# Attention of a two-block model: each head's weights divided in the head's own step, the output projection's parts at three places of a step

## The chip, the cores and the metric

The kernel runs on one core of a Trainium2 chip. The metric is the device time of one execution in microseconds (us), the median of several runs. The core has five engines that each work through their own list of instructions and wait for one another by semaphores: TensorE (PE, matmuls and transposes, with the weight loads PEld beside them), VectorE (DVE), ScalarE (ACT), GpSimd (POOL) and SyncE (SP, which issues most DMAs).

## The reference, cut to what matters

Two blocks are computed on a sequence of 512 tokens of 1024 channels, all in float32: a block with a Mamba-2 layer and an attention layer, then a block with two gated feed-forward layers and a second mixer. The change is in the attention layer:

```
def causal_block_attention(q_nope, q_rope, k_nope, k_rope, v):
    for i in range(S // Q_BLOCK):            # four blocks of 128 queries
        s = (q_nope . k_nope + q_rope . k_rope) * scale      # keys up to the block's end
        p = softmax(where(mask, s, -inf))
        outs.append(einsum('bhqk,bkhd->bqhd', p, v[:, :kv_len]))

def mla_mixer(...):                          # 16 heads, q and k of 96, v of 64
    o = causal_block_attention(q_nope, q_rope, k_nope, k_rope, v)
    o = o.reshape(Bsz, S, MLA_HEADS * V_HEAD) * silu(gate)
    return o @ w_out                         # 1024 x 1024
```

## The kernel before

All weight matrices come in units of at most 128x1024 numbers, 512 KB, through four buffers `raw`. A unit is split into a high part `wr` (on ACT, for a few units on DVE, L1494) and a low part `wl` (DVE, L1499, for the units of attention POOL), three buffers each; activations are split likewise into `XR` and `XL`. A float32 product is three matmuls, R by R, R by L and L by R (`three`, L743 to L745).

Attention is a loop of 18 **steps**, h = 0 to 17, written out on each engine. Head h gets its scores in step h and its transposes in step h + 2, so that steps 16 and 17 only finish heads 14 and 15. What each engine does in step h, in its order:

- PE: `turn_most(h-2)` transposes two of the three pieces of head h-2's weights `PP` (8 transposes, L960, into PSUM banks 5 and 6); `scores(h)` (banks 2, 3 and 4, L955 with the mask L956); `turn_rest(h-2)`, the third piece (2 transposes, again into bank 5, which the first piece must have left); `project(h)`, a part of the query and key projections for the heads of the next group, from a table `head_steps`: one tile of queries (9 matmuls of 512 columns), of keys (6) or both (15), and none from step 13 on; the parts of the output projection that `OUT_PARTS` names for h; and in odd steps from 3 on `values(j)` for heads h-3 and h-2, 16 matmuls (L984) into bank 7.
- ACT: `turned(h-2)`, three copies out of banks 5, 6 and 5 into `PT` (L1341); the division of blocks 0 to 2 of head h-1's weights by their sums (three multiplications by the reciprocal, L1356, after a wait on `s_tot`); the four exponentials of head h (L1365, with the sums), after a wait on `s_low`; in some steps the high part of a weight unit; in odd steps the high part of the output pair (`XR` from `OT`, L1186).
- DVE: the reciprocal of head h-1's sums (L1911, after a wait for its four exponentials); the row maxima of head h (four, L1919) and their negative (L1922, `s_low`); block 3 of head h-1's weights times the reciprocal (L1927); the evictions of `project(h)` into `QT` (three or four instructions for a tile of queries) and `KH` (two for a tile of keys), each time preceded by the casting of a unit where one is due; in odd steps the gated output `OT` (L1936) and, after ACT's high part, the low part `XL` (L1515).

`turn_most(h)` on PE waits for both halves of the division (`s_pwa`, `s_pwd`), `turn_rest(h)` for ACT's copy of the first piece (`s_pt`), `scores(h+1)` for the exponentials of head h (`s_exp`), which empty the same banks.

`OUT_PARTS` names pairs (n, t): the three matmuls of input tile t for output tile n, which need the output pair t. Before, the parts stand after `project(h)` in steps 13 to 16, ahead of `turn_most` in step 17, and after the loop (key 18). The rest of the output projection follows.

## Time and profile before

| what | us |
|---|---|
| median of 3 runs | 1834.27 (1833.46 to 1834.52) |
| the profiled execution's own time | 1834.76 |
| its span, first to last instruction | 1833.0 |
| attention, from the first score (496.20) to the end of the last parts (626.40) | 130.20 |
| PE busy in that stretch | 126.93 |
| DVE busy, ACT busy in it | 94.37, 83.08 |

The span is the stretch between the first and the last instruction that the profiler recorded; the time of the execution has 1.8 us more. A busy PE is a PE that has a matmul in flight: matmuls overlap, so one of 512 columns is listed with 0.39 us though the next starts 0.23 us after it. For that reason gaps on PE are best read from starts.

A row of a stretch gives the stretch, its length, the busy us and instructions of PE, PEld, DVE, ACT and POOL, the granted clock of TensorE as a share of 2.4 GHz, the DMA engines' busy share and GB/s. A row of a timeline gives start, duration, engine, line, operation, what it writes and reads, and how many instructions are merged in it; in brackets stands the idle time before it and what ended it.

### The profile page before, as it was taken

The page shows a single profiled execution, that of the slowest core. Times are in us where ns is not written, and L with a number is a line of the kernel's source. Part 1 is how long each engine was busy: PE and PEld are TensorE (multiplying, and loading weights), DVE is VectorE, ACT ScalarE, POOL GpSimd, SP SyncE. Part 2 cuts the span into 40 slices and gives each one's busy share as a digit, 9 for nine tenths or more (in the row PEclk, how much of TensorE's full clock was granted, in tenths as well). Part 3 has the DMA queues.
Part 4 walks back from the last instruction along what each step waited for, and adds up shares of the span by engine and source line. Part 5 has one row for each costly group of instructions (what it writes and reads, how often), then busy time and mean ns, then how long its engine had stood idle before and what let it go on. Part 6 is the DMA issues. An engine that isn't in the chain of part 4 may idle for free.

```text
span 1833.0 us, 21200 instructions
## 1 busy us (share of the span) xinstructions
PE 1804.8 (98%) x8390; PEld 1458.3 (80%) x8390; DVE 1041.9 (57%) x1511; ACT 725.3 (40%) x1198; POOL 49.6 (3%) x108
## 2 busy tenths in 40 slices
PE   8999999999999999999999999999999999999998
PEld 6767777888766788888888888888888888888887
DVE  7888887557587565444433356554444554444334
ACT  4876776434366543323222333222222332232221
POOL 1001010000210000000000000000000000000000
PEclk9999999999999999999999999999999999999999
DMA  4221222322210123333333323332332323333331
GB/s 168 79 70 58 81 70 70 103 93 82 86 47 24 60 79 109 99 92 103 86 103 99 121 77 96 97 104 92 95 101 92 101 94 93 103 93 91 104 96 55
DMA packets 48194, 163.44 MB, mean 89 GB/s; under 512 B 5344, under 2 KB 7776, under 8 KB 48096
## 3 DMA queue, kind: packets, MB, share of 16 engines
q1 hardware_dynamic: 47088, 161.24, 28.4%
q8 instruction: 67, 1.10, 0.3%
q10 hardware_dynamic: 1008, 0.85, 0.1%
q14 instruction: 31, 0.25, 0.0%
HBM read 159.97 MB, written 2.10 MB: 88 GB/s over the span
## 4 chain that ended last, share of the span: by engine, by line
PE 94%; DVE 4%; ACT 1%; issue 1%; DMA 0%; DVEq 0%; ACTq 0%
PE pb L743 28%; PE pb L744 28%; PE pb L745 28%; PE pb L846 2%; PE pb L955 2%; PE pb L960 1%; PE pb L984 1%; PE pb L1115 1%; PE pb L1117 1%; PE pb L1116 1%; DVE wl L1499 1%; PE pb L757 0%; DVE CV L1670 0%; PE pb L1125 0%; PE pb L811 0%
## 5 line engine op out<-in xcount | busy, mean ns | idle before, releaser
L743 PE MATMUL pb<-XR,wr 128*128 128x512 f32 x1584 | 625.8, 395 | 8.4 <-DVE XL L1517 8.4
L744 PE MATMUL pb<-XL,wr 128*128 128x512 f32 x1584 | 618.4, 390 | 0.0
L745 PE MATMUL pb<-XR,wl 128*128 128x512 f32 x1584 | 618.2, 390 | 0.0
L1499 DVE TENSOR_TENSOR wl<-raw,wr 128x1024 fp32r<-128x1024 f32 (+1 forms) x297 | 358.3, 1206 | 355.6 <-ACT wr L1173 354.8
L1173 ACT ACTIVATE wr<-raw 128x1024 fp32r<-128x1024 f32 (+1 forms) x295 | 305.5, 1036 | 314.6 <-PE pb L745 288.9
L743 PEld LDWEIGHTS pb<-XR,wr 128*128 128x128 f32 x1584 | 298.4, 188 | 72.8 <-issue 11.5
L745 PEld LDWEIGHTS pb<-XR,wl 128*128 128x128 f32 x1584 | 298.1, 188 | 62.9
L744 PEld LDWEIGHTS pb<-XL,wr 128*128 128x128 f32 x1584 | 298.4, 188 | 60.5
L743 PE MATMUL pb<-ffn2HR,wr 128*128 128x512 f32 (+1 forms) x198 | 72.5, 366 | 0.0
L744 PE MATMUL pb<-ffn2HL,wr 128*128 128x512 f32 (+1 forms) x198 | 72.3, 365 | 0.0
L745 PE MATMUL pb<-ffn2HR,wl 128*128 128x512 f32 (+1 forms) x198 | 72.3, 365 | 0.0
L743 PE MATMUL pb<-ffn1HR,wr 128*128 128x512 f32 x176 | 68.5, 389 | 0.0
L744 PE MATMUL pb<-ffn1HL,wr 128*128 128x512 f32 x176 | 68.5, 389 | 0.0
L745 PE MATMUL pb<-ffn1HR,wl 128*128 128x512 f32 x176 | 68.5, 389 | 0.0
L1182 ACT ACTIVATE SQ<-H 128x512 f32<-128x512 f32 x34 | 21.5, 631 | 92.3 <-DVE H L1681 47.6
L1670 DVE SCALAR_TENSOR_TENSOR CV<-U,vec,CV 128x512 f32<-128x512 f32 x72 | 54.1, 752 | 2.5
L1401 ACT ACTIVATE ffn2HR<-ffn2UP 128x512 fp32r<-128x512 f32 x22 | 13.9, 633 | 97.1 <-DVE ffn2UP L2004 97.1
L743 PE MATMUL pb<-YR,wr 128*128 128x512 f32 x128 | 50.0, 391 | 0.0
L745 PE MATMUL pb<-YR,wl 128*128 128x512 f32 x128 | 49.8, 389 | 0.0
L744 PE MATMUL pb<-YL,wr 128*128 128x512 f32 x128 | 49.8, 389 | 0.0
L1401 ACT ACTIVATE ffn1HR<-ffn1UP 128x512 fp32r<-128x512 f32 x22 | 13.9, 633 | 90.4 <-DVE ffn1UP L2004 90.4
L1759 DVE TENSOR_TENSOR LL<-LL,CB 128x1024 f32<-128x1024 f32 (+1 forms) x64 | 48.4, 819 | 0.7 <-ACT LL L1238 0.7
(337 smaller groups left out, 2248.2 us busy)
## 6 DMA issues: line engine op xcount, KB each, us to landing
raw<-in_ffn_in SPq DMA_DIRECT2D x88, 512.0 KB, 3.5
raw<-in_mix_in SPq DMA_DIRECT2D x48, 512.0 KB, 3.5
raw<-in_ssm_in SPq DMA_DIRECT2D x40, 512.0 KB, 3.3
raw<-in_ffn_out SPq DMA_DIRECT2D x32, 512.0 KB, 3.5
raw<-in_ffn_out SPq DMA_DIRECT2D x16, 384.0 KB, 3.2
raw<-in_mla_in SPq DMA_DIRECT2D x11, 512.0 KB, 3.3
raw<-in_ssm_out_a SPq DMA_DIRECT2D x8, 512.0 KB, 3.3
raw<-in_ssm_out_b SPq DMA_DIRECT2D x8, 512.0 KB, 3.3
```

Of the source, the lines that this page charges most:

```text
L743: e.matmul(o, r, xr, start=first, stop=False)
L744: e.matmul(o, r, xl, start=False, stop=False)
L745: return e.matmul(o, l, xr, start=False, stop=last)
L846: m = e.matmul(y[64 * p:64 * p + 64, 128 * k:S], XD[:, k, j, 64 * p:64 * p + 64], LL[q % 2][:, p, 512 * k:512 * k + S - 128 * k], start=k ...
L955: e.matmul(o[:, at:at + n], q[:, 128 * i:128 * i + 128], kh[:, 0:n], start=True, stop=False)
L960: m = e.transpose(o[:, at + 128 * (i - k):at + 128 * (i - k) + 128], PP[h % 3][:, POFF[i] + 128 * k:POFF[i] + 128 * k + 128], ident[:, :])
L1173: e.activation(wr[j % NS][:, 0:width(j)], raw[j % NR][:, 0:width(j)], ACT.Copy).then_inc(s_hi, 1)
L1182: e.activation(SQ[i][:, :], src, ACT.Square, scale=gain).then_inc(s_sq, 1)
L1401: e.activation(HRS[f][:, t, :], UPS[f][t % 2][:, :], ACT.Copy).then_inc(s_hhi, 1)
L1499: e.tensor_tensor(wl[j % NS][:, 0:width(j)], raw[j % NR][:, 0:width(j)], wr[j % NS][:, 0:width(j)].bitcast(F32), ALU.subtract).then_inc(s_ ...
L1670: e.scalar_tensor_tensor(out=cv, in0=u[:, k:k + S], scalar=col("conv_w", 4 * ch + k), in1=cv, op0=ALU.mult, op1=ALU.add).then_inc(then(s_c ...
L1759: m = e.tensor_tensor(x, x, CB[g % 2][:, OFF[k]:OFF[k] + d].unsqueeze(1).to_broadcast([128, 2, d]), ALU.mult)
```

## The change

In a head's step, its own weights are now divided, not those of the head before. On ACT the three multiplications come behind the four exponentials of the same head, after a wait for the reciprocal of these sums; on DVE the reciprocal and the multiplication of block 3 come behind the evictions of `project(h)`. Secondly `OUT_PARTS` now names three places of a step: 0 ahead of `turn_most`, 1 between `scores` and `turn_rest`, 2 after `project`. The parts of steps 13 to 15 stay in place 2; of step 16's four, two stand between `turn_most` and `turn_rest`; step 17 gets its two ahead of `turn_most` as before and two more, (2, 0) and (2, 1), between its transposes; eight of ten are left behind the loop. The number of instructions of each kind is the same.

```
-OUT_PARTS = {13: [(0, 0), (0, 1)], 14: [(0, 2), (0, 3), (0, 4)], 15: [(0, 5), (1, 0), (1, 1)],
-             16: [(1, 2), (1, 3), (1, 4), (1, 5)], 17: [(0, 6), (1, 6)],
-             18: [(2, 0), (2, 1), (2, 2), (2, 3), (0, 7), (1, 7), (2, 4), (2, 5), (2, 6), (2, 7)]}
+OUT_PARTS = {(13, 2): [(0, 0), (0, 1)], (14, 2): [(0, 2), (0, 3), (0, 4)], (15, 2): [(0, 5), (1, 0), (1, 1)],
+             (16, 1): [(1, 2), (1, 3)], (16, 2): [(1, 4), (1, 5)], (17, 0): [(0, 6), (1, 6)], (17, 1): [(2, 0), (2, 1)],
+             (18, 0): [(2, 2), (2, 3), (0, 7), (1, 7), (2, 4), (2, 5), (2, 6), (2, 7)]}
...
@@ PE, attention @@
             for h in range(18):
-                if h == 17:
-                    out_parts(h)
+                out_parts(h, 0)
                 if h >= 2:
                     turn_most(h - 2)
                 if h < 16:
                     scores(h)
+                out_parts(h, 1)
                 if h >= 2:
                     turn_rest(h - 2)
                 if h < 16:
                     project(h)
-                if h < 17:
-                    out_parts(h)
+                out_parts(h, 2)
                 if h >= 3 and h % 2 == 1:
                     values(h // 2 - 1)
-            out_parts(18)
+            out_parts(18, 0)
...
@@ ACT, attention @@
-                if 1 <= h <= 16:
-                    pp, sm = PP[(h - 1) % 3], st4[(h - 1) % 3]
-                    w.wait_ge(s_tot, h)
-                    for i in range(3):
-                        p = pp[:, POFF[i]:POFF[i] + 128 * (i + 1)]
-                        m = e.activation(p, p, ACT.Copy, scale=sm[:, 3, i:i + 1])
-                    m.then_inc(s_pwa, 1)
                 if h < 16:
...
                         e.activation(pp[:, POFF[i]:POFF[i] + n], PB[b][:, at:at + n], ACT.Exp, bias=sm[:, 1, i:i + 1],
                                      scale=SCALE, accum_out=sm[:, 2, i:i + 1]).then_inc(s_exp, 1)
+                    w.wait_ge(s_tot, h + 1)
+                    for i in range(3):
+                        p = pp[:, POFF[i]:POFF[i] + 128 * (i + 1)]
+                        m = e.activation(p, p, ACT.Copy, scale=sm[:, 3, i:i + 1])
+                    m.then_inc(s_pwa, 1)
...
@@ DVE, attention @@
-                if 1 <= h <= 16:
-                    sm = st4[(h - 1) % 3]
-                    w.wait_ge(s_exp, 4 * h)
-                    e.reciprocal(sm[:, 3, :], sm[:, 2, :]).then_inc(s_tot, 1)
...
-                if 1 <= h <= 16:
-                    pp, sm = PP[(h - 1) % 3], st4[(h - 1) % 3]
-                    p = pp[:, POFF[3]:POFF[3] + 512]
-                    w.wait_ge(s_tot, h)
-                    e.tensor_scalar(p, p, sm[:, 3, 3:4], None, ALU.mult).then_inc(s_pwd, 1)
                 if h < 16:
                     project(h)
+                    pp, sm = PP[h % 3], st4[h % 3]
+                    p = pp[:, POFF[3]:POFF[3] + 512]
+                    w.wait_ge(s_exp, 4 * h + 4)
+                    e.reciprocal(sm[:, 3, :], sm[:, 2, :]).then_inc(s_tot, 1)
+                    w.wait_ge(s_tot, h + 1)
+                    e.tensor_scalar(p, p, sm[:, 3, 3:4], None, ALU.mult).then_inc(s_pwd, 1)
```

ACT, steps 1 and 2, before: `PP0` and `PP1` are the weights of heads 0 and 1, `PT0` head 0's transposed weights.

```order
L1365 ACTIVATE PP1,st41<-pb2,st41 128x512 [waits s_low]
L1365 ACTIVATE PP1,st41<-pb3,st41 128x384
L1365 ACTIVATE PP1,st41<-pb3,st41 128x128
L1365 ACTIVATE PP1,st41<-pb4,st41 128x256
L1341 ACTIVATE PT0<-pb5 128x512 [waits s_turn]
L1341 ACTIVATE PT0<-pb6 128x512 [waits s_turn]
L1341 ACTIVATE PT0<-pb5 128x256 [waits s_turn]
L1356 ACTIVATE PP1<-PP1,st41 128x128 [waits s_tot]
L1356 ACTIVATE PP1<-PP1,st41 128x256
L1356 ACTIVATE PP1<-PP1,st41 128x384
L1365 ACTIVATE PP2,st42<-pb2,st42 128x512 [waits s_low]
```

The same place after the change (L1356 is now the exponential, L1361 the multiplication, L1339 the copy of a turned piece):

```order
L1356 ACTIVATE PP1,st41<-pb2,st41 128x512 [waits s_low]
L1356 ACTIVATE PP1,st41<-pb3,st41 128x384
L1356 ACTIVATE PP1,st41<-pb3,st41 128x128
L1356 ACTIVATE PP1,st41<-pb4,st41 128x256
L1361 ACTIVATE PP1<-PP1,st41 128x128 [waits s_tot]
L1361 ACTIVATE PP1<-PP1,st41 128x256
L1361 ACTIVATE PP1<-PP1,st41 128x384
L1339 ACTIVATE PT0<-pb5 128x512 [waits s_turn]
L1339 ACTIVATE PT0<-pb6 128x512 [waits s_turn]
L1339 ACTIVATE PT0<-pb5 128x256 [waits s_turn]
L1356 ACTIVATE PP2,st42<-pb2,st42 128x512 [waits s_low]
```

Head 1's three multiplications moved from behind to ahead of the three copies of head 0's transposes.

DVE, step 1, before (`st40`, `st41` hold the maxima, sums and reciprocals of heads 0 and 1):

```order
L1911 RECIPROCAL st40<-st40 128x4 [waits s_exp]
L1919 TENSOR_REDUCE st41<-pb2 128x1 [waits s_sc]
L1919 TENSOR_REDUCE st41<-pb3 128x1 [waits s_sc]
L1919 TENSOR_REDUCE st41<-pb3 128x1
L1919 TENSOR_REDUCE st41<-pb4 128x1 [waits s_sc]
L1922 TENSOR_SCALAR st41<-st41 128x4 [waits s_dve_step]
L1927 TENSOR_SCALAR PP0<-PP0,st40 128x512 [waits s_tot]
L1494 CAST wr2<-raw1 128x640 [waits s_raw1,s_hi]
L1886 TENSOR_TENSOR QT0<-pb0,TQ 96x512 [waits s_qp]
L1887 TENSOR_TENSOR QT0<-pb0,TA 32x512
L1889 TENSOR_TENSOR QT4<-pb0,TS 32x512
```

DVE from the same place after the change, the end of step 0 and step 1 but for its last three rows:

```order
L1920 RECIPROCAL st40<-st40 128x4 [waits s_exp]
L1922 TENSOR_SCALAR PP0<-PP0,st40 128x512 [waits s_tot]
L1911 TENSOR_REDUCE st41<-pb2 128x1 [waits s_sc]
L1911 TENSOR_REDUCE st41<-pb3 128x1 [waits s_sc]
L1911 TENSOR_REDUCE st41<-pb3 128x1
L1911 TENSOR_REDUCE st41<-pb4 128x1 [waits s_sc]
L1914 TENSOR_SCALAR st41<-st41 128x4 [waits s_dve_step]
L1490 CAST wr2<-raw1 128x640 [waits s_raw1,s_hi]
L1882 TENSOR_TENSOR QT0<-pb0,TQ 96x512 [waits s_qp]
L1883 TENSOR_TENSOR QT0<-pb0,TA 32x512
L1885 TENSOR_TENSOR QT4<-pb0,TS 32x512
L1898 TENSOR_TENSOR KH0<-pb1,RK 64x512 [waits s_unit]
```

The multiplication of head 0's block 3 moved ahead of the maxima of head 1, into step 0; in step 1 the reciprocal stays behind the evictions of the projection, as before.

PE, step 16 from its start, before: the transposes of head 14 (`PP2`), then the step's first two parts.

```order
L960 MATMUL pb5<-ident,PP2 128x128 [waits s_pwa,s_pwd]
L960 MATMUL pb5<-ident,PP2 128x128 x3
L960 MATMUL pb6<-ident,PP2 128x128 x4
L960 MATMUL pb5<-ident,PP2 128x128 [waits s_pt]
L960 MATMUL pb5<-ident,PP2 128x128
L743 MATMUL pb1<-XR,wr1 128x512
L744 MATMUL pb1<-XL,wr1 128x512
L745 MATMUL pb1<-XR,wl1 128x512
```

The same place after the change:

```order
L959 MATMUL pb5<-ident,PP2 128x128 [waits s_pwa,s_pwd]
L959 MATMUL pb5<-ident,PP2 128x128 x3
L959 MATMUL pb6<-ident,PP2 128x128 x4
L742 MATMUL pb1<-XR,wr1 128x512
L743 MATMUL pb1<-XL,wr1 128x512
L744 MATMUL pb1<-XR,wl1 128x512
L742 MATMUL pb1<-XR,wr1 128x512
L743 MATMUL pb1<-XL,wr1 128x512
L744 MATMUL pb1<-XR,wl1 128x512
L959 MATMUL pb5<-ident,PP2 128x128 [waits s_pt]
L959 MATMUL pb5<-ident,PP2 128x128
```

Two parts, six matmuls, moved between the first two pieces of head 14's transposes and the third.

## Rows read from the trace of the kernel before

**Rows 1.** The page's first part: engine, busy us, share of the span, instructions.

```profile
PE 1804.8 (98%) x8390; PEld 1458.3 (80%) x8390; DVE 1041.9 (57%) x1511; ACT 725.3 (40%) x1198; POOL 49.6 (3%) x108
```

**Rows 2.** Busy time by stretch: two after long PE gaps, then attention.

```profile
111.60:115.00 3.40, 3.40 (x12) 2.79 (x13) 2.52 (x5) 1.54 (x4) 0.00 (x0) 0.61 0.43 154
167.25:171.00 3.75, 3.75 (x21) 1.92 (x21) 1.80 (x3) 2.69 (x4) 0.00 (x0) 1.00 0.00 0
496.20:626.40 130.20, 126.93 (x685) 85.66 (x684) 94.37 (x194) 83.08 (x238) 10.17 (x5) 1.00 0.11 33
```

**Rows 3.** Waits of PE in attention: us in total, times, longest.

```profile
PE pb L960 <- ACT PT L1341: 1.6, 3, 0.9
```

**Rows 4.** Timeline of PE, steps 2 to 5: start, duration, engine, line, operation.

```profile
509.10 1.03 PE L960 MATMUL pb<-ident,PP 128*128 128x128 f32 x8
...
512.52 0.39 PE L960 MATMUL pb<-ident,PP 128*128 128x128 f32 x2
512.66 0.47 PE L743 MATMUL pb<-CQ,wr 128*128 128x512 f32 x1
...
514.58 0.39 PE L745 MATMUL pb<-CQ,wl 128*128 128x512 f32 x1
515.11 1.09 PE L960 MATMUL pb<-ident,PP 128*128 128x128 f32 x8
...
520.98 2.37 PE L984 MATMUL pb<-PT,VT 128*64 128x512 f32 x16
523.28 1.09 PE L960 MATMUL pb<-ident,PP 128*128 128x128 f32 x8
...
528.14 0.40 PE L745 MATMUL pb<-CK,wl 128*128 128x512 f32 x1
528.86 1.06 PE L960 MATMUL pb<-ident,PP 128*128 128x128 f32 x8 [0.32 <-issue]
```

**Rows 5.** Timeline of ACT, steps 1, 3 and 14.

```profile
506.39 1.31 ACT L1356 ACTIVATE PP<-PP,st 128x128 f32<-128x128 f32 x3 [2.85 <-DVE st L1911]
508.31 0.69 ACT L1365 ACTIVATE PP<-pb,st 128x512 f32<-128x512 f32 x1 [0.61 <-DVE st L1922]
...
510.34 1.09 ACT L1341 ACTIVATE PT<-pb 128x512 f32<-128x512 f32 x2
...
519.29 1.30 ACT L1356 ACTIVATE PP<-PP,st 128x128 f32<-128x128 f32 x3
520.49 0.67 ACT L1365 ACTIVATE PP<-pb,st 128x512 f32<-128x512 f32 x1
...
597.82 1.49 ACT L1341 ACTIVATE PT<-pb 128x512 f32<-128x512 f32 x3
```

**Rows 6.** Timeline of DVE, steps 1 to 3.

```profile
506.18 0.18 DVE L1911 RECIPROCAL st<-st 128x4 f32<-128x4 f32 x1
506.39 1.68 DVE L1919 TENSOR_REDUCE st<-pb 128x1 f32<-128x512 f32 x4
...
512.56 0.18 DVE L1911 RECIPROCAL st<-st 128x4 f32<-128x4 f32 x1
...
515.57 0.68 DVE L1886 TENSOR_TENSOR QT<-pb,TQ 96x512 f32<-96x512 f32 x1
...
517.71 0.18 DVE L1911 RECIPROCAL st<-st 128x4 f32<-128x4 f32 x1
...
521.08 0.69 DVE L1886 TENSOR_TENSOR QT<-pb,TQ 96x512 f32<-96x512 f32 x1 [0.89 <-PE pb L745]
```

**Rows 7.** Timeline of PE, third pieces of heads 12 and 14.

```profile
598.46 0.44 PE L960 MATMUL pb<-ident,PP 128*128 128x128 f32 x2 [0.45 <-ACT PT L1341]
...
611.15 0.44 PE L960 MATMUL pb<-ident,PP 128*128 128x128 f32 x2 [0.92 <-ACT PT L1341]
```

**Rows 8.** Timeline of DVE, last output pair and its low part.

```profile
619.64 0.69 DVE L1936 TENSOR_TENSOR OT<-pb,SG 128x512 f32<-128x512 f32 x1 [7.69 <-PE pb L984]
621.03 0.69 DVE L1515 TENSOR_TENSOR XL<-OT,XR 128x512 fp32r<-128x512 f32 x1 [0.70 <-ACT XR L1186]
```

More of the change, by code:

```diff
@@ L589, in build_in, with place_parts @@
     pieces = head_steps()
-    def place_parts(h):
-        for n, t in OUT_PARTS.get(h, ()):
+    def place_parts(h, place):
+        for n, t in OUT_PARTS.get((h, place), ()):
             if t == 0:
@@ L608, in build_in @@
     for h in range(18):
-        if h == 17:
-            place_parts(h)
+        place_parts(h, 0)
         if h >= 2:
@@ L617, in build_in @@
             bk.place(("sc", h, 1), 4, (s_sc, 4 * h + 4), (s_exp, 4 * h + 4))
+        place_parts(h, 1)
         if h >= 2:
@@ L621, in build_in @@
             place_project(h)
-        if h < 17:
-            place_parts(h)
+        place_parts(h, 2)
         if h >= 3 and h % 2 == 1:
             bk.place(("o", h // 2 - 1), 7, (s_val, h // 2), (s_ot, h // 2))
-    place_parts(18)
+    place_parts(18, 0)
     ring = Ring([4, 5, 6, 1, 2])
@@ L988, in _, with out_parts @@
         out_weights = {}
-        def out_parts(h):
-            for n, t in OUT_PARTS.get(h, ()):
+        def out_parts(h, place):
+            for n, t in OUT_PARTS.get((h, place), ()):
                 if t == 0:
@@ L1005, in attention @@
             for h in range(18):
-                if h == 17:
-                    out_parts(h)
+                out_parts(h, 0)
                 if h >= 2:
@@ L1015, in attention @@
                     project(h)
-                if h < 17:
-                    out_parts(h)
+                out_parts(h, 2)
                 if h >= 3 and h % 2 == 1:
                     values(h // 2 - 1)
-            out_parts(18)
+            out_parts(18, 0)
             for n in range(3, 8):
```

## The prediction

> **What bounds the kernel.** I read the page's first part, then busy time by stretch, then PE's waits in attention, and last the timelines of PE, ACT and DVE step by step. PE is busy 98% of the span [rows 1]. In attention it is busy 126.93 of 130.20 us, against 94.37 for DVE and 83.08 for ACT [rows 2]: whatever the change does on ACT and DVE counts only where PE then waits more or less, and no more than some 3 to 4 us can be won there. The page names few of PE's waits: 1.6 us for ACT's copies of turned pieces [rows 3]. Starts show more. Write T for the start of `turn_most` in a step. In step 2 the third piece starts 3.42 after T (509.10 to 512.52), the projection 0.14 later, and its matmuls follow each other by 0.24 (512.66 to 514.58 are eight of them). The last one of step 2 is through at 514.82, yet `turn_most` of step 3 starts at 515.11, 0.3 late [rows 4]: the division of head 1 was not done. After a step with keys only it is 0.49 late (528.14 plus 0.23 is 528.37; the start is at 528.86, and the bracket of that row shows 0.32 of it) [rows 4].
>
> **What goes away.** After the change a head's division ends in its own step, or early in the next, and `turn_most` needs it a whole step later. So these waits go: 0.3 in step 3, 0.49 in steps 5, 9 and 13 (one row stands for the three), 0.13 in step 15. In steps 16 and 17 there are no scores between the transposes: the third piece of head 14 starts 2.0 after its T, of which 1.1 is waiting for ACT's first copy (0.92 by the bracket) [rows 7], and in step 17 about 0.6 are lost in the same way. Two parts now stand in each of these places, six matmuls of 0.23, 1.38 us, which cover them. Step 14's wait for ACT, 0.6 (0.45 by the bracket) [rows 7], I treat below. Sum by starts: 0.3 + 1.5 + 0.1 + 0.6 + 1.1 + 0.6 = 4.2, and seven restarts after a wait at 0.05 each make it 4.5. By brackets and busy time alone it would be 2.7 (3.27 idle in the stretch less about 0.6 ahead of the first projection) [rows 2]; I take the starts, since a busy matmul hides 0.16 of each gap.
>
> **What comes in its place.** ACT works in its written order. The four exponentials of head h are now followed by the division of head h, which waits on `s_tot`. On DVE that reciprocal stands behind the evictions of `project(h)`, and those wait for PE to finish the projection, the last thing in step h. Queued behind the waiting division on ACT are the copies of head h-1's turned pieces, and for the first of them `turn_rest(h-1)` waits on PE, since the third piece goes to the same bank. Before, the division stood behind these copies. I follow that chain to the start of the third piece:
>
> Step 2. The reciprocal of head 1 is at 512.56, and nothing ahead of it on DVE changes its time [rows 6]. ACT starts its multiplications 0.21 after a reciprocal (506.18 to 506.39) [rows 5, 6], they hold it for 1.20 (519.29 to 520.49) [rows 5], and the third piece starts 0.64 after ACT begins the first copy (597.82 to 598.46) [rows 5, 7]. 512.56 + 0.21 + 1.20 + 0.64 = 514.61, where before it was 512.52 [rows 4]: **2.1 us**, once. Before, ACT took these copies at 510.34, right behind the exponentials [rows 5].
>
> Steps 3 and 7, behind a step with a tile of queries. From the end of the projection P: the eviction starts 0.19 later (at 521.08, 0.10 after `values` at 520.98, which start 0.09 after P) [rows 4, 6], three instructions take 2.14 (515.57 to 517.71) [rows 6], then 0.21 + 1.20 + 0.64 as above: P + 4.38. PE starts the next step at P, without the old wait, and wants the third piece at P + 3.42. So **0.95 each**, 1.9 for both.
>
> Steps 5, 9 and 13, behind a step with keys only. Here the odd step before it carries on. `values` take 2.30 (520.98 to 523.28) [rows 4]; if T is their end, the odd step's evictions (four instructions, 2.86, started at T - 2.2) end at T + 0.66, the reciprocal and block 3 take 0.6, `OT` starts at T + 1.27, ACT's high part at T + 2.07, the low part at T + 2.73 (the spacing of 1.39 from `OT` to low part is that of 619.64 to 621.03) [rows 8], the maxima at T + 3.34, the exponentials 1.92 later (506.39 to 508.31) [rows 5, 6], their end and the reciprocal 2.17 after that, at T + 7.43. Division and copy make it T + 9.48. The step lasts 5.09, so PE wants its third piece at T + 8.51: **0.95 each**, 2.9 for three. The exponentials then leave the score banks less than 0.1 before PE wants to write them again.
>
> Step 11: step 10 has a cast and a low part of an output unit ahead of its evictions on DVE. I take 1.4; its bounds are 0.95 (they are hidden) and 2.1 (as in step 2). Step 14: DVE's low part of a unit in step 13 now also follows ACT's division, 1.1 instead of 0.6. Step 15: 0.5. Odd steps with `values` give ACT 2.4 more, which covers the chain: 0 in steps 4, 6, 8, 10, 12 and 16.
>
> Behind the loop: part (0, 7) needs the low part of the last output pair, which ends 2.1 after `OT` begins (619.64 to 621.03 and 0.69) [rows 8], 2.2 after `values` end. Before, four parts (2.75) stood between; now two (1.38): **0.85**.
>
> Sum of the new waits: 2.1 + 1.9 + 2.9 + 1.4 + 1.1 + 0.5 + 0.85 = 10.7. Less 4.5 that go: **+6.2 us**. The instructions of each kind are as many as before, the parts and divisions cost nothing themselves. The profiled execution took 1834.76, 0.49 above the median; it would become 1841.0, and the median 1834.27 becomes **1840.5 us**. Behind attention PE is bound by its own matmuls, so the loss stays.
>
> **Rivals.**
>
> *The waits are half hidden.* If the reciprocal did not have to wait for all of the evictions, or the copies slipped in sooner, only step 2, 11 and 14 would keep their prices (4.6) and the seven others a third of theirs (2.1): 6.7 less 4.5, **+2.2, 1836.5 us**. For it: in the trace of before ACT idles 0.61 ahead of an exponential [rows 5], so that lists have slack. Against it: each link of the chain has its row.
>
> *Faster.* The copies reach PE in time everywhere, and only the old waits change. That needs the division to be through by P + 2.8 instead of P + 3.7, so the point is 0.9 us on ACT's list. All step waits are gone then, step 2's with them, and the result is -4.5 with (0, 7) still at 0.85: **-3.7, 1830.6 us**. It speaks for it that DVE and ACT are busy only 72% and 64% of the stretch [rows 2]; against it, that it is order and not load that makes the wait.
>
> *The clock falls.* Behind a PE gap of over 4 us at 107.4 to 111.6 the stretch that follows has a granted clock of 0.61, that is 1.2 GHz for most of its 3.4 us, and behind a gap of 2 us ahead of 167.25 it stays at 1.00 [rows 2]. Step 2's new gap of 2.1 us is like the second. If it acted like the first, half of some 3 us of work would be lost, **+1.5 on top, 1842.0 us**. The Trainium skill, TensorE: Matmul & The Clock Gate, section "HAM oscillation", warns that a PE left idle between bursts goes back to the low clock and starts each burst cold; by that rule every new gap might cost clock, while the row behind 167.25 says that one of this size does not.
>
> *Waits feed on themselves.* If the near ties at the score banks in steps 5, 9 and 13 go the wrong way, or step 11 costs 2.1, or the (0, 7) part delays the unit of output tile 3, some 3 us are added: **1843.5 us**.
>
> **How the numbers follow.** Forecast 0.68; waits feed on themselves 0.07; clock 0.06; half hidden 0.14; faster 0.05. A measurement of this kernel tells from no change what lies beyond 0.2%, 3.7 us. Faster by over that is half of its case and some room, 0.04; the half hidden case and the other half lie within it, 0.15; slower 0.81. The range runs from the half hidden case's upper side, 1836.8, to the self-feeding one, 1843.5; it leaves out the faster case and most of the half hidden one, about 0.15, and bounds the new waits from 7.0 to 13.7.
>
> **What would show it.** Right: ACT's three multiplications directly behind the exponentials with an idle time ended by DVE's reciprocal; PE's third pieces with gaps of near 1 us ended by ACT's copies in steps 3, 5, 7, 9, 11 and 13 and one of 2 us in step 2; `turn_most` without a wait in every step; no gap in steps 16 and 17; a wait of (0, 7) for the low part. Attention's stretch of 130.2 becomes 136.4. Wrong: third pieces on time, or a `turn_most` that still waits.

## The result: 7.6 us slower, 1.5 above the forecast

The changed kernel takes **1841.99 us** (median of four runs, 1840.72 to 1843.27), the kernel before 1834.35 (1833.46 to 1834.52): ratio 1.0040, 95% interval 1.0029 to 1.0052. Run again beside 21 runs of the kernel before, it took 1841.15 against 1834.28, ratio 1.0039 (1.0027 to 1.0052). It is slower, within the range (1836.8 to 1843.5), and 1.5 above the forecast of 1840.5 (0.65 by the second measurement). No run lies near 1841.99: of the nine, five took 1840.7 to 1841.2 and four 1843.2 to 1843.3.

The page of the changed kernel (span 1841.4 us), its busy times, against [rows 1]:

```profile
PE 1807.3 (98%) x8390; PEld 1459.8 (79%) x8390; DVE 1043.7 (57%) x1511; ACT 727.0 (39%) x1198; POOL 49.6 (3%) x108
```

As many instructions on each engine as before, and 2.5 us more of PE's busy time, though no matmul was added: a first hint that some of them ran slowly. The waits of PE in attention, against [rows 3] (us in total, times, longest):

```profile
PE pb L959 <- ACT PT L1339: 7.7, 9, 2.1
PE pb L742 <- DVE XL L1511: 0.6, 1, 0.6
```

Three waits of 1.6 us for ACT's copies of turned pieces have become nine of 7.7, and part (0, 7) waits for its low part. PE's timeline shows where (start, duration, engine, line, operation; steps 2 to 5 from their first transposes; in brackets PE's idle time and who ended it), against [rows 4]:

```profile
508.75 1.03 PE L959 MATMUL pb<-ident,PP 128*128 128x128 f32 x8
...
514.40 0.69 PE L959 MATMUL pb<-ident,PP 128*128 128x128 f32 x2 [2.07 <-ACT PT L1339]
...
516.17 0.63 PE L742 MATMUL pb<-CQ,wr 128*128 128x512 f32 x1
516.59 0.63 PE L743 MATMUL pb<-CQ,wr 128*128 128x512 f32 x1
...
518.32 1.03 PE L959 MATMUL pb<-ident,PP 128*128 128x128 f32 x8
...
522.72 0.44 PE L959 MATMUL pb<-ident,PP 128*128 128x128 f32 x2 [0.81 <-ACT PT L1339]
...
527.48 1.09 PE L959 MATMUL pb<-ident,PP 128*128 128x128 f32 x8
...
530.96 0.39 PE L959 MATMUL pb<-ident,PP 128*128 128x128 f32 x2
...
532.58 1.04 PE L959 MATMUL pb<-ident,PP 128*128 128x128 f32 x8
...
537.01 0.44 PE L959 MATMUL pb<-ident,PP 128*128 128x128 f32 x2 [0.52 <-ACT PT L1339]
```

Write T again for a step's first transposes. Step 2's third piece starts T + 5.65 instead of T + 3.42, step 3's T + 4.40, step 5's T + 4.43. Step 4's is on time (T + 3.48), and step 5 begins 5.10 after step 4, not 5.58: `turn_most` no longer waits. From 515.31 to 517.45 the projection's matmuls follow each other by 0.43 instead of 0.23.

ACT and DVE show the chain (same columns), against [rows 5, 6]:

```profile
512.56 1.31 ACT L1361 ACTIVATE PP<-PP,st 128x128 f32<-128x128 f32 x3 [1.93 <-DVE st L1920]
513.77 1.06 ACT L1339 ACTIVATE PT<-pb 128x512 f32<-128x512 f32 x2
...
520.88 1.30 ACT L1361 ACTIVATE PP<-PP,st 128x128 f32<-128x128 f32 x3 [3.33 <-DVE st L1920]
522.09 1.48 ACT L1339 ACTIVATE PT<-pb 128x512 f32<-128x512 f32 x3
...
535.17 1.31 ACT L1361 ACTIVATE PP<-PP,st 128x128 f32<-128x128 f32 x3 [0.24 <-DVE st L1920]
```

```profile
512.35 0.18 DVE L1920 RECIPROCAL st<-st 128x4 f32<-128x4 f32 x1
...
518.52 0.69 DVE L1882 TENSOR_TENSOR QT<-pb,TQ 96x512 f32<-96x512 f32 x1 [2.95 <-PE pb L744]
...
519.94 0.69 DVE L1885 TENSOR_TENSOR QT<-pb,TS 32x512 f32<-32x512 f32 x1
520.66 0.18 DVE L1920 RECIPROCAL st<-st 128x4 f32<-128x4 f32 x1
...
534.96 0.18 DVE L1920 RECIPROCAL st<-st 128x4 f32<-128x4 f32 x1 [0.77 <-ACT PP L1356]
```

ACT stands for 1.93 and 3.33 us in front of a division, and the copies that PE wants come right behind it. In step 2 the reciprocal at 512.35 frees the division, and PE has its third piece 2.05 later, at 514.40, as the chain said. In step 3 the first eviction starts at 518.52, the reciprocal at 520.66, the division at 520.88, the first copy at 522.09 and the third piece at 522.72: the sequence that the forecast wrote down as 2.14, 0.21, 1.20 and 0.64 measures 2.14, 0.22, 1.21 and 0.63. Step 5's longer chain holds too. With T = 527.48, the start of step 4, its reciprocal at 534.96, which waits for ACT's exponentials and not for an eviction, is at T + 7.48 (forecast 7.43), and the third piece at 537.01 is at T + 9.53 (forecast 9.48).

**A measure that can be compared.** The instructions ahead of attention are the same in all 14 profiles of this study, and yet attention's step 2 begins anywhere from 507.95 to 511.32. From the first score to T of step 2 it is 12.86 to 12.91 us in all of them, so the change costs nothing in steps 0 and 1. Behind the output projection PE multiplies with a column of ones (`ones`, L757 before, L756 after) to get the sums that the next layer's norm needs; I call these the m-sums. From the first of them to the end it is 1169.1 us before and after the change. So I compare profiles by **attention's length**, from T of step 2 to the start of the m-sums: 154.76 before (509.10 to 663.86), 163.54 after (508.75 to 672.29), **+8.78**. The second profile of the change gives 163.57. It is the only kernel with two profiles, so the 0.03 between them is all that is known of this measure's noise.

| from T of step | before | after | difference | forecast |
|---|---|---|---|---|
| 2 | 6.01 | 9.57 | +3.56 | +1.8 |
| 3 | 8.17 | 9.16 | +0.99 | +0.95 |
| 4, 8 and 12 together | 16.74 | 15.29 | -1.45 | -1.5 |
| 5, 7 and 9 together | 27.16 | 30.26 | +3.10 | +2.85 |
| 6 and 10 together | 11.58 | 11.58 | 0.00 | 0 |
| 11 | 8.14 | 9.64 | +1.50 | +1.4 |
| 13 | 7.46 | 8.51 | +1.05 | +0.95 |
| 14 | 6.59 | 6.81 | +0.22 | +0.4 |
| 15 | 8.19 | 8.66 | +0.47 | +0.5 |
| 16 | 6.42 | 5.30 | -1.12 | -1.1 |
| 17, to the m-sums | 48.30 | 48.76 | +0.46 | +0.25 |
| all | 154.76 | 163.54 | +8.78 | +6.5, less 0.3 for restarts |

(In row 14 the forecast is 1.1 of new wait less 0.6 and 0.13 of old; in row 17, 0.85 less 0.6.) One row stands out, step 2, and the stretch behind its gap tells why. Windows of PE in the changed kernel (stretch, length, PE's busy time and instructions, granted clock, DMA share, GB/s):

```profile
514.40:518.32 3.92, 3.92 (x12) 0.57 0.00 0
...
518.32:672.29 153.97, 147.48 (x765) 1.00 0.15 45
```

The clock fell to 1.2 GHz for most of the 3.92 us behind the gap of 2.07 us. The same twelve matmuls take 2.36 at full clock (below), so the fall costs **1.56**, and step 2 without it is +2.00. Attention without it is +7.2, against +6.2 of the forecast.

### The profile page after: what moved, and what is told of

It is laid out like the page before. It is cut to its first block, busy times and chain, and to the rows that moved or that the text cites. A ratio compares the mean times of both kernels' runs of the same rounds, so it can differ in the third digit from the quotient of the medians.

```text
span 1841.4 us, 21200 instructions
## 1 busy us (share of the span) xinstructions
PE 1807.3 (98%) x8390; PEld 1459.8 (79%) x8390; DVE 1043.7 (57%) x1511; ACT 727.0 (39%) x1198; POOL 49.6 (3%) x108
## 4 chain that ended last, share of the span: by engine, by line
PE 90%; DVE 6%; ACT 3%; issue 1%; DMA 0%; DVEq 0%; ACTq 0%
PE pb L742 28%; PE pb L743 27%; PE pb L744 27%; PE pb L845 2%; ACT PP L1361 1%; PE pb L1113 1%; PE pb L1115 1%; PE pb L1114 1%; DVE wl L1495 1%; ACT PP L1356 1%; DVE st L1911 1%; PE pb L756 0%; DVE CV L1666 0%; DVE QT L1883 0%; PE pb L959 0%
```

## Which half of the change costs, and which gains

The experiments' kernels have other line numbers: PE's transposes are L962, scores L957, values L986; ACT's division L1349, copies L1342, exponentials L1369; DVE's reciprocal L1914, maxima L1934. They are the changed kernel with tables in place of its fixed rule. `divide(h)` holds ACT's wait and three multiplications, `total(h)` DVE's reciprocal, `divide_last(h)` its block 3; `ALL` is 0 to 15. On ACT:

```
                if 1 <= h <= 16 and h - 1 not in ACT_OWN:
                    divide(h - 1)
...
                if h in ACT_OWN:
                    divide(h)
```

The first place stands behind the copies and ahead of the exponentials, the second behind the exponentials. `DVE_OWN` does the same on DVE: a head that isn't in it has its reciprocal at the start of the next step and its block 3 behind that step's maxima, as before. The diffs are against the change, in which both tables are `ALL`. First the change again.

> The changed kernel once more. Its four times so far lie in two pairs, 1840.7 and 1843.3, and the profile of 1843.3 shows a granted clock of 0.57 from 514.40 to 518.32, behind step 2's wait of 2.07 us. Theory A (queue order plus clock): the pairs are executions without and with that fall; if this profile is of a 1840.7 run, its clock at that place is 1.00 and its step 3 starts some 1.8 us earlier; if it is of a 1843.3 run, the fall is there again. Rival: the two levels have another place, then a profile of either level shows the same clock there.

The profiled execution took 1843.15 us, one of the upper group again, and the fall is there again: a clock of 0.57 from 514.36 to 518.29, behind a gap of 2.08 us. No execution of the lower group was profiled, so the expectation's question stays open.

**The division alone**, with the parts where they were:

```
-             (16, 1): [(1, 2), (1, 3)], (16, 2): [(1, 4), (1, 5)], (17, 0): [(0, 6), (1, 6)], (17, 1): [(2, 0), (2, 1)],
-             (18, 0): [(2, 2), (2, 3), (0, 7), (1, 7), (2, 4), (2, 5), (2, 6), (2, 7)]}
+             (16, 2): [(1, 2), (1, 3), (1, 4), (1, 5)], (17, 0): [(0, 6), (1, 6)],
+             (18, 0): [(2, 0), (2, 1), (2, 2), (2, 3), (0, 7), (1, 7), (2, 4), (2, 5), (2, 6), (2, 7)]}
```

> The division moved as in the change, the output parts left where they were. Theory A (ACT's copies of turned pieces stand behind a division that waits for DVE): the waits of the third pieces in steps 2, 3, 5, 7, 9, 11, 13 stay, the waits of steps 16 and 17 (1.7 us) come back and the one of part (0, 7) (0.85) goes: +7.0 against before, or +9 where the clock falls behind step 2. Rival B (the parts carry the loss): near the time of before, within 1 us.

1844.22 us, ratio 1.0052 (1.0039 to 1.0065). Attention's length is 162.63, +7.87, with steps 16 and 17 as before. That the median lies above the change's although attention is 0.9 shorter has its place, at least in the profiled execution (1844.68), ahead of attention: it enters step 2 at 511.32, 2.6 later than the change's, and 1.6 of that is a fall of the clock near 167 (next section).

**The parts alone**, each head's division in the next step as before:

```
-ACT_OWN = DVE_OWN = ALL
+ACT_OWN = DVE_OWN = ()
```

> Only the output parts moved, the division as before. Theory A: 1.7 us of waits in steps 16 and 17 go, 0.85 for part (0, 7) comes: -0.85, with one level of times and a clock of 1.00 throughout attention. Rival B (the parts carry the loss): +3 us or more.

1833.77 us, ratio 0.9998 (0.9989 to 1.0006). Attention 154.03, **-0.73**. The halves add: 7.87 - 0.73 = 7.14, and the whole change without its clock fall is 7.22. So the division is the whole loss and the parts are a small gain by attention's length, too small for the times of whole runs to tell (the interval contains 1); the parts' gain is smaller than what they cover (1.1 and 0.47) because of (0, 7). The changed kernel's end of attention, against [rows 7, 8]:

```profile
618.23 1.09 PE L959 MATMUL pb<-ident,PP 128*128 128x128 f32 x8
...
620.55 0.38 PE L959 MATMUL pb<-ident,PP 128*128 128x128 f32 x2
...
626.10 2.37 PE L983 MATMUL pb<-PT,VT 128*64 128x512 f32 x16
...
629.69 0.39 PE L744 MATMUL pb<-XR,wl 128*128 128x512 f32 x1
630.65 0.50 PE L742 MATMUL pb<-XR,wr 128*128 128x512 f32 x1 [0.58 <-DVE XL L1511]
```

Step 16's third piece starts without a gap, 2.32 after T, of which 1.38 are the two parts. Part (0, 7) starts 0.96 after the matmul ahead of it, not 0.23: 0.73 lost.

## Step 2 and the clock

**Head 1 alone divided in its own step**, all others in the next, parts as before:

```
-ACT_OWN = DVE_OWN = ALL
+ACT_OWN = DVE_OWN = (1,)
```

> The kernel before, but for head 1, whose division alone is done in its own step on ACT and DVE. Theory A: the third piece of head 0 in step 2 starts 2.1 us late, the 0.3 us wait ahead of step 3 goes: +1.8, and +3.6 in executions where the clock falls behind that wait; so two levels of times or the higher one. Rival: one wait of 2 us does not lower the clock, and all is +1.8 on one level.

1837.95 us, ratio 1.0016 (1.0007 to 1.0025), attention +3.32. Of eleven runs nine lie at 1837.8 to 1838.5 and two at 1835.8. The profiled one is of the nine. Windows of PE behind the gap of step 2, first of this kernel (gap 1.92), then of the division alone (gap 2.06):

```profile
514.50:518.42 3.92, 3.92 (x11) 0.56 0.00 0
```

```profile
516.96:519.32 2.36, 2.36 (x12) 1.00 0.00 0
```

The same work, 3.92 against 2.36, with a smaller gap ahead of the slower. The kernel with early reciprocals, in the next section, kept its clock too, and so it did behind a gap of 1.98 in its step 14. Its windows, behind 2.07 and behind 1.98:

```profile
513.88:516.24 2.36, 2.36 (x11) 1.00 0.00 0
```

```profile
605.77:613.00 7.23, 6.92 (x37) 1.00 0.13 54
```

So of six gaps of 1.92 to 2.08 us in attention, three took the clock down (both profiles of the change, and head 1 alone) and three did not. The prediction weighed two rows of this kind, a clock of 0.61 behind a gap over 4 us and 1.00 behind one of 2 us [rows 2], and took the second as the pattern. That second gap, 1.95 to 1.96 us ahead of the same instructions, stands in every profile of this study. Behind it the clock stayed at 1.00 in 12 of the 14 and fell in two, the division alone and the kernel with head 1 in the next step, below. The same stretch in the kernel before and in the division alone:

```profile
167.25:171.09 3.84, 3.83 (x21) 1.00 0.00 0
```

```profile
167.89:173.32 5.43, 5.43 (x21) 0.69 0.00 0
```

It costs 1.59 there (in the other one too, 167.60 to 173.03), and these two are the profiles that enter step 2 at 511.32 and 510.99, where the other twelve do so from 507.95 to 509.10. So the gap's length does not decide it: the same gap went either way. What does decide stays open. The Trainium skill, TensorE: Matmul & The Clock Gate, section "HAM oscillation", says that a PE left idle between bursts starts the next one cold. Its example has longer waits than these, so it does not say what a gap of 2 us does, and the prediction's "every new gap" is wider than the page. Here a cold start came behind three of the six gaps of this size in attention and behind two of the 14 ahead of it, and behind none of the shorter ones in attention (0.31 to 1.29 in the changed kernel, with a clock of 1.00 from 518.32 on).

**Head 1 in the next step, all others in their own** (on DVE all in their own):

```
-ACT_OWN = ALL
+ACT_OWN = (0, 2, 3, 4, 5, 6, 7, 8, 9, 10, 11, 12, 13, 14, 15)
```

> The change, but head 1's division on ACT stays behind the copies of head 0's turned pieces, as before. Theory A: step 2's wait of 2.2 us goes, and with it the clock's fall (1.6 us more); the waits of near 1 us in steps 3, 5, 7, 9, 13 and 14 and 1.5 in step 11 stay. +5.0 against before, with a clock of 1.00 throughout attention. Rival: if the fall had another cause than that gap, it is still there.

1841.16 us, ratio 1.0036 (1.0022 to 1.0050), attention +5.70: 3.1 less than the change's, of which 1.56 is the clock, and 0.7 more than I expected. Step 2 has no gap. Step 3 has a larger one, PE's timeline first and DVE's behind it:

```profile
516.71 1.03 PE L962 MATMUL pb<-ident,PP 128*128 128x128 f32 x8
518.08 1.12 PE L957 MATMUL pb<-KH,QT 128*128 128x512 f32 x2 [0.34 <-ACT PP L1369]
...
521.93 0.44 PE L962 MATMUL pb<-ident,PP 128*128 128x128 f32 x2 [1.03 <-ACT PT L1342]
```

```profile
517.12 0.69 DVE L1500 CAST wr<-raw 128x1024 fp32r<-128x1024 f32 x1
517.74 0.68 DVE L1892 TENSOR_TENSOR QT<-pb,TQ 96x512 f32<-96x512 f32 x1
```

The third piece comes at T + 5.22, not T + 4.40. DVE's evictions start at 517.74, right behind the cast and with no idle time, while in the changed kernel DVE waited 2.95 for PE there. Step 2's wait had given DVE time to catch up; take it away, and 0.8 of it returns one step later. A wait's price is not what its removal gives.

## ACT's list or DVE's?

The change moves the division on two engines. **ACT alone goes back** to the next step, DVE keeps the reciprocal and block 3 in their own:

```
-ACT_OWN = ALL
+ACT_OWN = ()
```

> The change, but ACT's division of every head stands behind the copies as before; the reciprocal and block 3 on DVE stay in the head's own step, the parts where the change puts them. Theory A (it is ACT's list that costs): no third piece waits in steps 2 to 13, so the time is that of the moved parts alone, -0.7, or down to -1.0 where block 3's earlier end helps turn_most. Rival (DVE's new order, which puts reciprocal and block 3 ahead of the output pair, costs too): +1 or more.

1834.74 us, ratio 1.0001 (0.9991 to 1.0010), attention 154.10, **-0.66**: as good as the parts alone (-0.73). Against the change without its clock fall (+7.22) that is 7.9 us less, so it is ACT's place in the list that costs, and DVE's new order by itself costs nothing.

**The other way to shorten the chain**: the reciprocal and block 3 ahead of the evictions in the even steps, all else as in the change:

```
+EARLY_R = (2, 4, 6, 8, 10, 12, 14)
...
+                    if h in EARLY_R:
+                        total(h)
+                        divide_last(h)
                     project(h)
-                    if h in DVE_OWN:
+                    if h in DVE_OWN and h not in EARLY_R:
                         total(h)
                         divide_last(h)
```

> The change, but in even steps from 2 on DVE takes the reciprocal and block 3 ahead of the evictions of the projection. Theory A (the division waits for DVE's evictions): the waits of the third piece in steps 3, 7 and 11 go (0.98, 0.98, 1.46), those of 5, 9 and 13, where the exponentials are last, stay at 1.0, and so does step 2's 2.2 with the fall of the clock: 3.4 us less than the change, +5.4 against before with the fall, +3.8 without. Rival (ACT's exponentials, not DVE's evictions, are last everywhere): the same time as the change.

1842.95 us, ratio 1.0050 (1.0034 to 1.0065), attention +7.81, 0.6 above the change without its clock fall, where I expected 3.4 less (this profile too kept its clock behind step 2). The steps behind the edit did shorten by a good 1 us: 8.14 from T of step 3, 8.13 of step 7 and 8.66 of step 11, for 9.16, 9.15 and 9.64. But PE waits elsewhere. PE's steps 12 and 14, then DVE's step 10 and 11:

```profile
584.70 1.09 PE L962 MATMUL pb<-ident,PP 128*128 128x128 f32 x8
...
589.84 0.44 PE L962 MATMUL pb<-ident,PP 128*128 128x128 f32 x2 [1.50 <-ACT PT L1342]
...
600.16 1.09 PE L962 MATMUL pb<-ident,PP 128*128 128x128 f32 x8
...
605.77 0.44 PE L962 MATMUL pb<-ident,PP 128*128 128x128 f32 x2 [1.98 <-ACT PT L1342]
```

```profile
577.88 0.18 DVE L1914 RECIPROCAL st<-st 128x4 f32<-128x4 f32 x1 [2.21 <-ACT PP L1369]
...
579.28 1.23 DVE L1505 TENSOR_TENSOR wl<-raw,wr 128x1024 fp32r<-128x1024 f32 x1
...
582.57 1.69 DVE L1934 TENSOR_REDUCE st<-pb 128x1 f32<-128x512 f32 x4
```

DVE now stands 2.21 us in front of the reciprocal, for ACT's exponentials, with a cast, a low part and the evictions behind it. Head 11's maxima begin at T + 6.53, in the changed kernel at T + 3.56 (579.51 to 583.07), and the third pieces of steps 12 and 14 are late (+1.7 and +1.2 against the change). Step 14 gets it through step 12's maxima, behind the same kind of wait: ACT's exponentials of head 13 start 2.16 ahead of T (598.00 to 600.16), in the changed kernel 3.31 (599.45 to 602.76). It is the change's own mistake made once more, on the other engine: a wait put ahead of work that does not need it.

## Which heads, and which parts

**Odd heads 3 to 15 in their own step**, the others in the next, parts as before. A second edit on ACT puts the high part of a weight unit (`hi`) ahead of the division, which among these heads acts in steps 5, 9 and 13:

```
-ACT_OWN = DVE_OWN = ALL
+ACT_OWN = DVE_OWN = (3, 5, 7, 9, 11, 13, 15)
...
-                if h in ACT_OWN:
-                    divide(h)
                 if h < 11 and h % 4 in (1, 2) or h == 13:
                     hi()
+                if h in ACT_OWN:
+                    divide(h)
```

> The kernel before, but heads 3, 5, ... 15 are divided in their own steps, whose values cover the wait; even heads and head 1 stay in the next step. Theory A: no third piece waits more than before, turn_most no longer waits in steps 5, 9, 13 (0.49 each) and 15 (0.1); of that the score banks give back up to 0.27 in each of three steps: -0.8 against before. Rival: a division in the own step costs in odd steps as well, +1 or more.

1833.69 us, ratio 0.9998 (0.9989 to 1.0006), attention **-0.72**. Its steps 4 and 5 on PE:

```profile
522.48 1.09 PE L962 MATMUL pb<-ident,PP 128*128 128x128 f32 x8
...
527.58 1.04 PE L962 MATMUL pb<-ident,PP 128*128 128x128 f32 x8
...
531.33 0.39 PE L962 MATMUL pb<-ident,PP 128*128 128x128 f32 x2
```

Step 5 begins 5.10 after step 4, not 5.58, and the third piece comes at T + 3.75 instead of T + 3.45: 0.3 of the 0.49 is given back to the exponentials in the score banks, so 0.2 stays in each of steps 5, 9 and 13. No run has the odd heads without the second edit, so what that edit gives is not known.

**Even heads in their own step**, parts as before:

```
-ACT_OWN = DVE_OWN = ALL
+ACT_OWN = DVE_OWN = (0, 2, 4, 6, 8, 10, 12, 14)
```

> The kernel before, but the even heads are divided in their own steps and the odd ones in the next, the counterpart of the run in which only odd heads moved (attention 0.7 us shorter). Theory A: the loss sits in the divisions of even heads, which stand ahead of the copies of odd steps with no values before them: third pieces wait near 1 us in steps 3, 5, 7, 9 and 13, 1.5 in step 11, step 2 does not wait and the clock stays at 1.00: attention 7 to 8 us longer than before. Rival: the loss comes from each moved division alike, then near half of the whole, 3 to 4 us.

1839.98 us, ratio 1.0030 (1.0020 to 1.0041), attention +5.51, of the 7.87 that the whole division costs. Most of the loss comes with the even heads, as the chain says: an even head's projection is the last thing in its step, while behind an odd head's stand the values. Head 1, which is in neither set, costs 1.76 without its clock fall. The three add up to 6.55 (5.51 + 1.76 - 0.72), so 1.3 comes only with all heads moved together, or from the high part of a unit, which the odd heads' run had ahead of the division. I had expected 7 to 8. Its steps 4 to 5 on PE:

```profile
524.46 1.09 PE L962 MATMUL pb<-ident,PP 128*128 128x128 f32 x8
...
530.04 1.06 PE L962 MATMUL pb<-ident,PP 128*128 128x128 f32 x8 [0.32 <-issue]
...
534.06 0.44 PE L962 MATMUL pb<-ident,PP 128*128 128x128 f32 x2 [0.40 <-ACT PT L1342]
```

From T of step 4 to the third piece of step 5 it is 9.60, in the changed kernel 9.53 (527.48 to 537.01): the chain is as long as there. But here `turn_most` is late by the old 0.49, so that only 0.57 is new. I had counted both in full three times. And step 14's old wait of 0.6 is gone: in step 13 no division stands between ACT's copies and its exponentials any more, and ACT's high part of a unit starts 1.30 ahead of T of step 14 (598.80 to 600.10) instead of 0.11 (594.25 to 594.36).

**One part instead of two between step 17's transposes**, no division moved (both tables empty), so that three parts cover the low part of the last output pair:

```
-             (16, 1): [(1, 2), (1, 3)], (16, 2): [(1, 4), (1, 5)], (17, 0): [(0, 6), (1, 6)], (17, 1): [(2, 0), (2, 1)],
-             (18, 0): [(2, 2), (2, 3), (0, 7), (1, 7), (2, 4), (2, 5), (2, 6), (2, 7)]}
+             (16, 1): [(1, 2), (1, 3)], (16, 2): [(1, 4), (1, 5)], (17, 0): [(0, 6), (1, 6)], (17, 1): [(2, 0)],
+             (18, 0): [(2, 1), (2, 2), (2, 3), (0, 7), (1, 7), (2, 4), (2, 5), (2, 6), (2, 7)]}
```

> The kernel before with the output parts as in the change, but for one part only, (2, 0), between step 17's transposes, and (2, 1) back behind the loop. Theory A: one part, 0.69 us, covers step 17's wait as well as two, and part (0, 7) has three parts ahead of it and waits 0.15 instead of 0.85: attention 1.4 us shorter than before, where both parts together gave 0.7. Rival: step 17 needs both parts, then no gain over 0.7.

1833.06 us, ratio 0.9992 (0.9983 to 1.0001), attention **-1.39**; (0, 7) starts 0.31 after the matmul ahead of it (620.17 to 620.48), so it loses 0.08 instead of 0.73.

**Both together**: odd heads 3 to 15, and one part in step 17.

> Odd heads from 3 on divided in their own steps, even heads and head 1 as before, with the parts as in the run before it (one part between step 17's transposes). Theory A: the gains are at different places and add: 0.7 and 1.4, attention 2.1 us shorter than before, a time 2 us under it. Rival: head 15's earlier division already takes away part of the end's waits, then 1.5.

**1832.44 us**, ratio to the kernel before 0.9988 (0.9980 to 0.9997), attention -2.13 (-0.72 and -1.39 make -2.11). It is the fastest kernel of the study, some 9 us below the change. Against the kernel before, its interval excludes 1, but the gain lies within the 0.2% that I had taken as the bound of what can be told. One wait for ACT's copies is left, in step 14 (0.6 by starts):

```profile
593.47 1.09 PE L962 MATMUL pb<-ident,PP 128*128 128x128 f32 x8
...
597.57 0.44 PE L962 MATMUL pb<-ident,PP 128*128 128x128 f32 x2 [0.45 <-ACT PT L1342]
```

**DVE's low part of step 13 behind `OT`'s**, to take that wait away:

```
-                if h == 13:
-                    lo()
...
                     x_lo(3, j, OT, None)
+                if h == 13:
+                    lo()
```

> The run with odd heads and one part together, and in step 13 DVE makes the low part of the unit for output tile 2 behind the low part of the output pair instead of ahead of the pair's gating. Theory A: step 14's third piece waits 0.6 us because that unit's low part holds the output pair and so ACT's copies; moved, the wait goes and nothing needs the unit before step 17: attention 2.7 us shorter than before, against 2.1 without this edit. Rival: the maxima of head 14 come later by the low part's 1.15 and step 15 waits instead: no gain over 2.1.

1832.66 us, ratio 0.9990 (0.9981 to 0.9999), attention -2.04: no gain over the one before, where I expected 0.6. The rival was right. Steps 14 and 15:

```profile
593.67 1.09 PE L962 MATMUL pb<-ident,PP 128*128 128x128 f32 x8
...
597.15 0.39 PE L962 MATMUL pb<-ident,PP 128*128 128x128 f32 x2
...
599.45 1.03 PE L962 MATMUL pb<-ident,PP 128*128 128x128 f32 x8
600.96 1.10 PE L957 MATMUL pb<-KH,QT 128*128 128x512 f32 x2 [0.47 <-ACT PP L1369]
```

Step 14's wait is gone (third piece at T + 3.48), and step 15 waits 0.47 for the exponentials at the score banks; its third piece comes at T + 4.13, 0.7 later than without. The same work on DVE is late either for the copies or for the maxima.

## Why the prediction came out as it did

**What bounds the kernel**: right. Behind attention nothing moved (1169.1 us both times), and inside it the difference is waits of PE, apart from 1.56 of clock.

**What goes away**, forecast 4.5: 4.1 by starts. Step 3's 0.3, the three of 0.49, step 15's 0.13, step 14's 0.6 and step 16's 1.1 are as said; step 17's 0.6 is 0.47 (from the transposes to the values, 623.53 to 626.10, it is 2.57, less 1.38 of parts 1.19, where it was 1.66, 615.56 to 617.22). The **"seven restarts after a wait at 0.05 each"** were wrong: five of the seven are waits of `turn_most`, and behind these the third piece is no later than else (before, T + 3.45 in step 5, T + 3.48 in step 4, which starts on time). Only a third piece that waited costs 0.05 more: the next matmul starts 0.19 behind it (522.72 to 522.91) instead of 0.14 (before, 512.52 to 512.66). Of these waits two go and eight come, so restarts are a loss of some 0.3 (an estimate, six times 0.05) and no gain.

**What comes in its place**, forecast 10.7: 10.9 by starts, made of step 2 2.23 (said 2.1), steps 3 and 7 0.98 each and 5, 9 and 13 1.01 to 1.03 (said 0.95), 11 1.46 (1.4), 14 0.98 (1.1), 15 0.48 (0.5) and part (0, 7) 0.73 (0.85). Each gap stands where it was put and is ended by the releaser that was named. For steps 2, 3, 5, 7, 9 and 13 the forecast had a chain of rows. Steps 11, 14 and 15 (3.0 of the 10.7) it put down without one, so that their fit is partly luck; step 11's 1.4 was picked between 0.95 and 2.1, and in the trace DVE's evictions start there 0.69 after T behind a low part (580.20), where in step 3 it is 0.20, which is the 0.49 that it waits more. In steps 5, 9 and 13 the near tie at the score banks went the wrong way by 0.27, but that lies inside the wait for the copies and costs nothing of its own. Undoing ACT's move alone takes the 7.9 us back, which shows that the division ahead of the copies is the cause.

**Sum.** 10.9 less 4.1 is 6.8, and attention without the clock is 7.2 longer; the restarts are 0.3 of the last 0.4. Against +6.2 the terms were 0.2 too low on one side and 0.4 too high on the other.

**The clock.** The rival was priced at +1.5 on top of the forecast, with a chance of 0.06; its mechanism came true in both profiled executions of the change, at 1.56. So the forecast's mechanism and this rival's both hold. That the median of 1841.99 meets the rival's 1842.0 is luck, since it lies midway between two pairs of runs. The step that failed is the one that read the row behind 167.25 [rows 2] as what a gap of 2 us does: behind that very gap the clock fell in two of 14 profiles. The trace of before also had a third gap of this kind, which was not weighed: 2.31 us ahead of 1826.95, with a clock of 0.50 behind it, though PE had already idled 1.24 us and done only eight one-column products ahead of it. The same gap is in all 14 profiles, with a clock of 0.50 to 0.57 over the 4 us behind it. One row was no ground for so low a chance.

**The rivals "half hidden" and "faster"** are out: no third piece of steps 3, 5, 7, 9, 11 or 13 waited less than priced, and none came in time. **"Waits feed on themselves"** did not happen in the change; it did in the kernel with the early reciprocals, and a milder form in the one without step 2's wait.

**Open.** The change's nine timed runs fall in two groups, near 1840.9 (five) and 1843.2 (four), and both profiled ones are of the upper. The fall in step 2 (1.56) would explain a part of the 2.4 between them if the lower group kept its clock there, as two of the eleven runs with head 1 alone suggest; no profile of such a run exists here, so it is argued and not shown. The rival is the gap near 167, whose fall costs as much (1.59) and can come in any of these kernels. Two of the 21 runs of the kernel before, which has no gap in step 2, took 1836.7 with a mean clock of 0.996 over the whole run, the other 19 at most 1835.0 with 0.997. The kernel with no gap in step 2 has two groups as well (1839.5 to 1839.9 and 1842.4), and the profile of its upper one has the fall near 167.

## What to carry to other kernels

ACT and DVE work off their lists in order. The Trainium skill, Perfetto Trace Analysis, section "Tensor Engine Instruction (MATMUL, LD_WEIGHTS)", calls ACT and DVE strict FIFO, and the traces agree: in step 3 the copy written behind the division starts at 522.09, after ACT stood 3.33 us in front of that division. So before an instruction is moved up "to be ready earlier", ask what it waits for and what stands behind it that does not need it. Here moving ACT's division up removed waits of 0.3 to 0.5 us at the transposes and put ones of 1 to 2 us at the copies; only with the heads whose projection isn't the last work of a step did attention get shorter, by 0.7. Work of the bottleneck engine that waits for nothing, such as two parts of the output, is better cover for a gap than an earlier result of another engine, as long as what it is taken from keeps three.

## What I had not expected of the hardware

- A PE gap of about 2 us between dense stretches takes the granted clock from 1.00 to 0.56 or 0.57 over the following 3.9 us in some cases (gaps 2.07, 2.08, 1.92) and leaves it at 1.00 in others (2.06, 2.07, 1.98). Even the same gap of 1.95 to 1.96 us ahead of the same instructions did both, 2 times and 12 times. The price is 1.56 to 1.59 us each time, on top of the gap itself.
- The first 500 us of the same instructions differ by up to 3.4 us between the profiles of this study (507.95 to 511.32 at step 2), on one core with nothing beside it; 1.6 of that is the clock's fall near 167 in two of them. Medians of kernels that differ by 1 us in attention can stand in the wrong order by that, and the length of the changed stage told them apart.
